# Gate and up projections of a SwiGLU block: seven block products in place of eight, in 36 of 44 units

## The reference

```
x = x + 0.5 * swiglu(rmsnorm(x, norm_ffn1), ffn1_w_in, ffn1_w_out)
x = x + token_mix(rmsnorm(x, norm_mix), ...)        # HGRN2 heads, FoX attention, paged cache
x = x + 0.5 * swiglu(rmsnorm(x, norm_ffn2), ffn2_w_in, ffn2_w_out)
y = rmsnorm(x, norm_final)

def swiglu(h, w_in, w_out):                          # w_in 1024 x 5632, w_out 2816 x 1024
    a, b = jnp.split(h @ w_in, 2, axis=-1)           # a: gate, b: up, each 2816 wide
    return (jax.nn.silu(a) * b) @ w_out
```

## Time and profile before

| | |
|---|---|
| median of 3 runs | 1288.49 us (1287.96 to 1290.75) |
| profiled execution, span | 1288.7 us |
| PE busy, share of the span | 1261.1 us, 98% |
| PE weight loads | 1179.9 us, 92% |
| DVE busy | 589.6 us, 46% |
| ACT busy | 477.0 us, 37% |
| POOL busy | 108.2 us, 8% |
| matmuls with 128 x 272 output at L2163 | 5568 in gate/up and mix input, 2112 in FFN outputs |
| DMA | 172.37 MB, mean 134 GB/s |

### The profile page before, as it was taken

The page is one execution under the profiler, slowest core; times in us unless marked ns, Lnnn a source line. Parts: engine busy times, 40 slices in busy tenths (PEclk is TensorE's granted clock), DMA queues, the critical chain, the costliest instruction groups (busy, mean ns, idle before and its releaser), DMA issues.

```text
span 1288.7 us, 29970 instructions
## 1 busy us (share of the span) xinstructions
PE 1261.1 (98%) x12437; PEld 1179.9 (92%) x12437; DVE 589.6 (46%) x1103; ACT 477.0 (37%) x772; POOL 108.2 (8%) x247
## 2 busy tenths in 40 slices
PE   9999999999999999998989999999999999999998
PEld 8999999999999999996656666699999999999998
DVE  6644432244354433246756576645434422434433
ACT  6543221122233112434866776634222311222233
POOL 1000000000013100000222422122000000000000
PEclk9999999999999999999989999999999999999999
DMA  7323422232322342354798999532333322233211
GB/s 202 98 80 84 139 91 65 66 88 75 123 90 66 114 138 74 100 193 147 243 356 317 336 342 374 167 99 67 98 98 98 114 82 65 66 97 106 82 42 70
DMA packets 186602, 172.37 MB, mean 134 GB/s; under 512 B 11377, under 2 KB 149138, under 8 KB 186514
## 3 DMA queue, kind: packets, MB, share of 16 engines
q1 hardware_dynamic: 185346, 167.47, 41.3%
q0 software_dynamic: 1104, 3.67, 0.8%
q10 hardware_dynamic: 64, 0.02, 0.0%
HBM read 162.19 MB, written 8.93 MB: 133 GB/s over the span
## 4 chain that ended last, share of the span: by engine, by line
PE 90%; DVE 3%; DMA 2%; issue 2%; ACT 2%; SPq 1%; POOL 0%; ACTq 0%; DVEq 0%; POOLq 0%
PE ps L2163 78%; DMA d_keys<-in_cache_k 2%; PE ps L990 2%; PE ps L1075 2%; PE ps L1090 2%; SPq L612 1%; PE ps L915 1%; PE ps L955 1%; PE ps L935 1%; PE ps L753 1%; ACT d_keysT L1335 1%; PE ps L2327 0%; PE ps L2146 0%; PE ps L2132 0%; PE ps L896 0%
## 5 line engine op out<-in xcount | busy, mean ns | idle before, releaser
L2163 PE MATMUL ps<-n_hi,w_hi 128*128 128x272 f32 x1856 | 387.1, 288 | 2.0 <-DVE w_lo L2679 0.8
L2163 PE MATMUL ps<-n_hi,w_lo 128*128 128x272 f32 x1856 | 386.7, 288 | 0.0
L2163 PE MATMUL ps<-n_lo,w_hi 128*128 128x272 f32 x1856 | 385.2, 288 | 0.0
L2374 ACT ACTIVATE w_hi<-w_raw 128x2048 fp32r<-128x2048 f32 (+2 forms) x76 | 156.0, 2052 | 540.6 <-PE ps L2163 540.6
L2163 PEld LDWEIGHTS ps<-n_hi,w_hi 128*128 128x128 f32 x1856 | 293.0, 188 | 2.8 <-issue 2.6
L2163 PEld LDWEIGHTS ps<-n_lo,w_hi 128*128 128x128 f32 x1856 | 292.7, 189 | 0.0
L2163 PEld LDWEIGHTS ps<-n_hi,w_lo 128*128 128x128 f32 x1856 | 290.7, 189 | 0.0
L2551 DVE TENSOR_TENSOR w_lo<-w_raw,w_hi 128x2048 fp32r<-128x2048 f32 (+2 forms) x75 | 191.6, 2555 | 49.5 <-ACT w_hi L2374 49.5
L2163 PE MATMUL ps<-g_hi,w_lo 128*128 128x272 f32 x704 | 149.0, 289 | 0.0
L2163 PE MATMUL ps<-g_hi,w_hi 128*128 128x272 f32 x704 | 148.9, 288 | 0.0
L2163 PE MATMUL ps<-g_lo,w_hi 128*128 128x272 f32 x704 | 148.4, 288 | 0.0
(11 more groups left out here) (363 smaller groups left out, 1232.6 us busy)
## 6 DMA issues: line engine op xcount, KB each, us to landing
w_raw<-in_ffn_w_in SPq DMA_DIRECT2D x87, 512.0 KB, 5.0
d_keys<-in_cache_k SPq DMA_DIRECT2D x128, 256.0 KB, 5.2
d_values<-in_cache_v SPq DMA_DIRECT2D x124, 256.0 KB, 6.1
w_raw<-in_w_in_mix SPq DMA_DIRECT2D x28, 512.0 KB, 4.8
w_raw<-in_ffn_w_out SPq DMA_DIRECT2D x16, 768.0 KB, 5.5
w_raw<-in_ffn_w_out SPq DMA_DIRECT2D x16, 640.0 KB, 4.8
w_raw<-in_w_out_mix SPq DMA_DIRECT2D x8, 512.0 KB, 4.9
suffix_scratch<-d_log_f_sums SPq DMA_DIRECT2D x32, 64.0 KB, 2.1
```

The costliest lines, as they stand in the source:

```text
L2163: mm = pe.matmul(bank(4 * j + 2 * t + half), wp, xp[:, k, half * HALF:(half + 1) * HALF], start=(k == 0 and wp is w[0] and xp is x_hi), st ...
L2374: nc.scalar.activation(w_hi[j][:, 0:kt * UC], w_raw[j][:, 0:kt * UC], ACT.Copy).then_inc(w_hi_ready, 1)
```

## The change

A gate/up unit can be written as a 2 x 2 block product. The weights have four blocks of 128 columns x 512 rows: A11, A12 (gate, lower and upper half of K) and A21, A22 (up, likewise). The input has four blocks of 512 rows x 272 tokens: B11, B12 (lower K, first and second token half) and B21, B22. Taken straight this is eight block products of 4 contraction tiles x 3 passes = 12 matmuls each. The Winograd form of Strassen's scheme needs seven, made of sums:

- weights, for every unit: S3 = A11 + A21, S1 = A21 + A22, S2 = A11 + S1, S4 = A12 + S2 (signs are folded into the inputs and into a factor -1 on the gated tile);
- inputs, once for each FFN: U1 = B11 - B12, T3 = B22 - B12, T2 = U1 + B22, T4 = T2 - B21;
- products, in PE's order and with their PSUM names: alpha = A11 B11, gamma = S1 U1, beta = S2 T2, delta = S3 T3, eps = A22 T4, then S4 B22 added onto gamma and A12 B21 added onto alpha.

Each sum is made in fp32 and then split into high and low parts like any operand, so for each such unit the split covers 7 blocks of 512 elements a partition (3584) instead of 4 (2048). Five DVE additions combine the products (`z_step`), after ACT has copied alpha and gamma out before they are added to (`z_kept`). Since sums mix token halves, the norm's 1/rms must already be in the input: `build_full` makes x times gain times rstd, `build_sum` the sums, `build_hi` (ACT) and `build_lo` (DVE) the parts. That takes room, so `CHUNKS` becomes (4, 6, 6, 6): the first 4 units of each FFN keep the old form, the other 18 take the new one, and there are 16 output units with kt = 4 or 6 in each FFN instead of 8 with kt = 12 or 10. The number of matmuls in output units stays the same. The loops of the new units are written out instead of run as `Fori` loops. The rest of the diff moves buffers and merges semaphores. Input building is placed in DVE's and ACT's order around the gate steps of units 2 and 3 and the first output units; the weight work for the first new unit of a chunk stands behind the third output unit.

```diff
-CHUNKS = (12, 10)
+CHUNKS = (4, 6, 6, 6)
+FIRST, GT = CHUNKS[0], max(CHUNKS)
...
+        Z_BANKS = ((0, 2, 1, 3, 4), (5, 7, 6, 1, 3))
...
+            def seven_products(unit_n, j, z, n, f):
+                alpha, gamma, beta, delta, eps = Z_BANKS[j]
+                before = 5 * (z - 1)
+                def product(out, a, b, more=False):
+                    for k in range(KB):
+                        for n_pass, (w, x) in enumerate(((z_hi, b_hi[f][:, b, k, :]), (z_hi, b_lo(f, b)[:, k, :]),
+                                                          (z_lo, b_hi[f][:, b, k, :]))):
+                            mm = pe.matmul(bank(out), w[j][:, a, k * P:(k + 1) * P], x, ...
+                pe.wait_ge(z_los, 4 * z + 1)
...
+                product(alpha, A11, B11).then_inc(z_product, 1)
+                pe.wait_ge(z_los, 4 * z + 2)
...
+                product(gamma, S1, U1).then_inc(z_product, 1)
+                pe.wait_ge(z_los, 4 * z + 3)
+                if n:
+                    pe.wait_ge(z_step, before + 2)
...
+                product(beta, S2, T2).then_inc(z_product, 1)
+                if n:
+                    pe.wait_ge(z_step, before + 4)
...
+                product(delta, S3, T3).then_inc(z_product, 1)
+                pe.wait_ge(z_los, 4 * z + 4)
...
+                product(eps, A22, T4).then_inc(z_product, 1)
+                pe.wait_ge(w_lo_ready, unit_n + 1)
+                pe.wait_ge(z_copied, 2 * z + 2)
...
+                product(gamma, S4, B22, more=True).then_inc(z_product, 1)
+                pe.wait_ge(z_copied, 2 * z + 1)
...
+                product(alpha, A12, B21, more=True).then_inc(mm_done, 1)
...
+            def seven_products_scalar(unit_n, z, f, n, q, last_kt):
+                if n:
+                    z_silu_first(unit_n - 1, z - 1)
+                if last_kt is None:
+                    block_hi_raw(unit_n + 1, z + 1)
...
+                if n:
+                    z_gated_hi(f, n - 1, q - 1)
+                if last_kt is None:
+                    block_hi_raw_up(unit_n + 1, z + 1)
+                act.wait_ge(z_product, 6 * z + 1)
+                nc.scalar.activation(z_kept[:, 0, :], bank(alpha), ACT.Copy).then_inc(z_copied, 1)
+                if last_kt is None:
+                    block_hi_sums(unit_n + 1, z + 1)
+                act.wait_ge(z_product, 6 * z + 2)
+                nc.scalar.activation(z_kept[:, 1, :], bank(gamma), ACT.Copy).then_inc(z_copied, 1)
+                if last_kt is None:
+                    block_hi_last(unit_n + 1, z + 1)
+                act.wait_ge(z_step, 5 * z + 5)
+                nc.scalar.activation(z_gate[:, 1, :], z_gate[:, 1, :], ACT.Silu).then_inc(z_silu, 1)
...
+            def block_sums(unit_n, z):
+                j = unit_n % 2
+                dve.wait_ge(w_landed[j], unit_n // 2 * 32 + 32)
+                dve.wait_ge(mm_done, unit_n - 1)
+                nc.vector.tensor_tensor(z_sum[j][:, S3:S1 + 1, :], z_raw[j][:, 0:4:3, :],
+                                        z_raw[j][:, 2:3, :].to_broadcast([P, 2, BLOCK]), ALU.add).then_inc(z_sums, 1)
...
+            def seven_products_vector(unit_n, z, f, n, q, last_kt, before):
+                if blocks:
+                    block_sums(nxt, z + 1)
+                if n:
+                    z_gated(z - 1, q - 1)
+                else:
+                    before()
+                if blocks:
+                    block_sum_two(nxt, z + 1)
+                if n:
+                    z_gated_lo(f, n - 1, q - 1)
+                if blocks:
+                    block_sum_four(nxt, z + 1)
+                    block_lo_gate(nxt, z + 1)
...
+                dve.wait_ge(z_product, 6 * z + 3)
+                dve.wait_ge(z_copied, 2 * z + 1)
+                nc.vector.tensor_tensor(z_part[:, 0, :], z_kept[:, 0, :], bank(beta), ALU.subtract).then_inc(z_step, 1)
+                if blocks:
+                    block_lo_sums(nxt, z + 1)
...
+                nc.vector.tensor_tensor(z_part[:, 1, :], z_part[:, 0, :], bank(delta), ALU.add).then_inc(z_step, 1)
+                if blocks:
+                    block_lo_two(nxt, z + 1)
...
+                nc.vector.tensor_tensor(z_up[:, 1, :], z_part[:, 1, :], z_kept[:, 1, :], ALU.add).then_inc(z_step, 1)
+                if blocks:
+                    block_lo_up(nxt, z + 1)
+                dve.wait_ge(z_product, 6 * z + 5)
+                nc.vector.tensor_tensor(z_up[:, 0, :], z_part[:, 1, :], bank(eps), ALU.add).then_inc(z_step, 1)
+                if blocks:
+                    block_lo_four(nxt, z + 1)
+                dve.wait_ge(z_product, 6 * z + 6)
+                nc.vector.tensor_tensor(z_gate[:, 1, :], z_part[:, 0, :], bank(gamma), ALU.add).then_inc(z_step, 1)
...
@@ DVE's ffn, chunk 0 @@
+                        build_full(f, norm, range(KB))
+                        gate_step(p0 + 1, 0, q0 + 2, f, 2, kt)
+                        build_full(f, norm, range(KB, KD))
+                        gate_step(p0 + 1, 1, q0 + 3, f, 3, kt)
+                        build_sum(f, U1, b_full(f, B11), b_12[:, :, :], ALU.subtract)
+                        build_sum(f, T3, b_full(f, B22), b_12[:, :, :], ALU.subtract)
+                        build_sum(f, T2, b_full(f, U1), b_full(f, B22), ALU.add)
+                        dve.wait_ge(mm_done, 2 * (p0 + pairs))
+                        build_sum(f, T4, b_full(f, T2), b_full(f, B21), ALU.subtract)
+                        build_lo(f, TURN_ORDER[:2])
...
+                    if c < LAST_CHUNK:
+                        add_out(p0, 0, 0, 0.5, False)
+                        split_lo(p0 + 1, 0, kt)
+                        if c == 0:
+                            build_lo(f, TURN_ORDER[2:3])
+                        add_out(p0, 1, 0, 0.5, False)
+                        split_lo(p0 + 1, 1, kt)
+                        if c == 0:
+                            build_lo(f, TURN_ORDER[3:5])
+                        add_out(p0 + 1, 0, 1, 0.5, False)
+                        nxt, z = 2 * (p0 + 2), wino_index(f, c + 1)
+                        block_sums(nxt, z)
...
+                        def before(pair=p0 + 1, first=c == 0):
+                            add_out(pair, 1, 1, 0.5, False)
+                            if first:
+                                build_lo(f, TURN_ORDER[5:])
```

376 lines of the change are left out of this document (284 added, 92 removed).

## The result

The changed kernel takes 1251.22 us (median of 4 runs, 1249.46 to 1256.24) against 1289.62 us (1287.96 to 1291.13) for the kernel before: a ratio of 0.971, 95% interval 0.968 to 0.973. Forecast were 1244, with a range of 1235.5 to 1262. So the time lies in the range, 7 us above the forecast.

A forecast was written before the change was run, and what follows sets the result against it. PE was taken to bound the kernel: span 1288.7 - 54.1 saved + 7.5 first-chunk stalls + 0.55 page sums + 1.0 kernel's end + 1.0 product borders = 1244.6 us, median about 1244, range 1235.5 to 1262.

The forecast's parts named there:

- The saving: 36 new units with 84 matmuls instead of 96, at 0.1253 us each: 54.1 us less, all on PE's path.
- The sum's term for product borders: 36 x 7 more small waits on PE between products, under 0.01 us each: 1.0 us added.
- DVE's account: DVE's instructions in one new unit: 9.6 us of PE's 10.53, or 9.95 with PSUM additions at 0.43 us.
- The first rival: DVE's instructions don't overlap, so a new unit takes DVE 11.0 us against 10.53: 1252 us, chance 0.10.
- Stall (a): First output unit of each FFN: PE waits for the gated tile's low part, 1.85 us.
- Stall (b): Third output unit of each FFN: PE waits for low weights behind DVE's input building, 0.95 us.
- Stall (c): Second new unit of each FFN: DVE begins late and ACT's copy of gamma comes late, 0.95 us.
- The page sums: End of FFN 1: low weights behind the gather wait and page sums come late for PE, 0.55 us.
- The kernel's end: Last output quarters: the token factors on DVE, ahead of the fourth quarter's add, set the distance; 0.9 to 1.0 us lost.
- Fewer stalls: Case that fewer stalls come than were counted: 1234.6 to 1238 us, chance 0.07.
- The product borders: Rival: each product border drains PE, up to 0.16 us each, 35 us in all; 1255 to 1279 us, chance 0.08.
- DVE as the bound: Rival: DVE slowed 1.5 times sets the pace, 1366 us; a loss from about 12.3 us a unit; chance 0.05.

The follow-up runs named there:

- the second run: The changed kernel timed once more with no edit: 1251.24 us, ratio 0.970.
- the better kernel: The changed kernel with the repairs together (page sums, gated tile, input sums, input low parts and ACT's order moved): 1247.63 us, ratio 0.967.
- the last experiment: Against the changed kernel, low weights of FFN 1's second last-chunk output unit made ahead of the last gated low part: 1250.49 us.

## Why the prediction came out as it did

**The saving.** 432 matmuls at PE's pace: right in kind, all of it on the path. Mis-sized by the pace of the new products, which I took from the old ones: 0.1261 us for 0.1253. The sum had 10.53 us a unit where 10.59 were found, 36 x 0.066 = 2.4 us. The sum's term for product borders (1.0 us) happened to stand there, with the wrong reason, and hid a part of the miss by luck: borders are free, the place of the input tiles isn't. The step from "12 in a row into one bank: that costs nothing" to the old pace for the new products looked at PSUM and at waits and not at what PE reads. That costs 1.4 us beyond the 1.0.

**DVE's account.** 9.6 us of instructions a unit forecast, 9.45 found and 0.2 of waiting for ACT (the laying-out had that wait), with 0.35 us for the additions that no row showed. Of the two ends that I had, 0.36 by likeness to SBUF and 0.43 by a neighbour, the likeness held. The neighbour was fed by ACT, which may be what set its 0.43. The first rival fell with the overlap of 0.08 us. The Trainium skill, "VectorE: DVE Perf Modes", "The DRAIN you can't avoid", has the next instruction wait until the pipeline is empty, apart from instructions that aren't held; this trace shows 0.08 us of overlap all through a new unit, behind additions that begin with a wait on PE and ahead of them. Taken for every instruction, the rule would have given the first rival, and the trace doesn't agree with it; it agrees with the exception. Whether these instructions are ones that aren't held, no run here tests.

**Stall (a).** Forecast 1.85, found 2.03 and 1.82. **Stall (b).** 0.95, found 1.23 in FFN 2 and 1.44 in FFN 1 of the second run. **Stall (c).** 0.95, found 0.64 and 0.65. The three were laid out by hand over 30 us of DVE's order and sum to 3.75 us an FFN; FFN 2 has 3.70. The experiments showed two mechanisms where I had one growing lateness: (a) and (b) are one debt, paid at whichever comes first. (c) is ACT's order on top of a lateness that DVE takes up in the first new unit itself: it goes with one swap on ACT, doesn't move when (b) is paid off, and grows by 1.2 us when DVE gets 1.2 us more to do. In FFN 2 it is 0.3 us less than forecast and (b) 0.28 more; that the sum came out to 0.05 us is luck.

**What I left out: the clock.** I priced a stall at its own length. In five of the eight profiled executions that have the changed kernel's stall (a) in FFN 1 and no addition to DVE, either (a) or the stall behind the page sums went with some 3 us at the 1.2 GHz level, 1.4 to 1.5 us lost. In the changed kernel's own it cost 1.5 us and took away (b): 4.2 us in FFN 1's first chunk for 3.75, 0.45 net.

**The page sums.** Forecast 0.55 us, found 2.19, and 2.98 in the second run. The chain was the right one, the moved start too. The failed term is the gather's 5.64 us, which I carried over as if it were fixed. It took 7.1 us here, since the new order on DVE puts low weights, and the loads behind them, beside it; the last experiment shows this. This is 1.46 of the 1.64 us missed. Most of the rest is the signal from DVE to PE: the low weights end at 376.05 and PE goes on at 376.40. The laying-out had 0.1 us for each such signal without saying so (18.5 less 18.05 is 0.45 and not 0.55, and 4.75 less 3.0 in (a) is 1.75 and not 1.85). I had asked what queues behind the moved step and not what runs beside it. In before an output unit of 15 us would have hidden such a difference; a unit of 9 us, already 0.55 us short, hides none of it.

**The kernel's end.** 0.9 to 1.0 forecast, 0.91 found, by the mechanism named.

**The mix stage.** I gave it nothing, not even a spread. It varies by 4 us from execution to execution, and 2.2 of the 6.1 us are this.

**The sum of the misses.** Pace 1.4, page sums 1.65, mix 2.2, clock less (b) 0.45: 5.7 of 6.1 us, and the slow second matmul behind each of six stalls is most of the rest. As for the median, the 1.9 us around the span belong in it: 1244.6 + 1.9 = 1246.5 was what my own sum said, against 1251.22.

**The rivals.** "Fewer stalls" was what the better kernel made of it, not the change. The product borders and DVE without overlap are refuted by their own rows. (The price of the borders, 35 us, would have left a fifth of the saving, not the third that the prediction says.) DVE as the bound didn't happen, and its break-even held when DVE was given that much work; the factor of 1.5 behind its price of 122 us was never tested.

## What to carry to other kernels

When the bottleneck gets less work, list what the old, longer stretches hid, and take each waiting chain by its worst reading, not by the one row at hand: a gather's price depends on what the new order puts beside it. Add up the order of every in-order engine from the unit that is late, since it's the order and not the busy share that stalls the others; a debt is removed by moving work to where there is slack, not by choosing which of its waits comes first. Several short stalls were better here than a long one of the same sum, since the clock fell only around stalls of some 2 us and more, and not around each of those.

## What the runs showed of the hardware

- The pace of matmuls of 272 fp32r columns depended on which input tile they read: from 10.36 to 10.64 us for 84, at full clock, with PE never idle. The old units had 0.1252 us each, the new 0.1261.
- Waits on PE that were already met cost nothing: eight more in a unit of 96 matmuls leave it at 12.03 us.
- Around stalls of PE in the FFNs of 1.98 to 2.98 us the granted clock sometimes fell to 0.50 for about 3 us, in 12 of 22 cases, between 0.5 us ahead of the stall's end and 1.2 us behind it. Of the two such stalls of the changed kernel's execution it fell behind the one of 2.03 us and not behind the one of 2.19, and behind one of 3.35 us in another execution it did not fall either. Around stalls of 1.85 us and less it never did in these runs. What decides in between isn't settled.
- POOL's instruction for an indirect gather took 1.21 us beside an idle DVE and 1.81 us beside DVE's low weights; with weight loads issued behind it, the rows landed 6.9 to 8.3 us after the release, and 5.4 to 5.6 with the loads issued ahead of it.
- DVE's instructions overlapped by 0.08 us throughout: 272 elements lasted 0.43 us and started 0.35 apart, 1024 lasted 1.22 and started 1.14 apart.
